# A hybrid attention and convolution layer: modulation rows, convolution taps and output products in another order, convolution sums in SBUF

## The reference, cut to what matters

```python
sc = silu(c)
mod = sc @ ada_w + ada_b
sh1, sc1, g1, sh2, sc2, g2 = split(mod, 6)
xn = rmsnorm(x, norm1_g) * (1.0 + sc1) + sh1
q, k, v, ca, cg = split(xn @ w_in)                     # 8 heads x 64, 512 conv channels
q, k = rmsnorm(q, q_norm_g), rmsnorm(k, k_norm_g)      # per head
y_attn = causal softmax(q k^T / 8 + rel_bias) v        # SEQ = 256: one block, all of it causal
a = causal_dwconv(ca * sigmoid(cg), conv_dw_w, conv_dw_b)   # 31 taps
a = silu(group_norm(a, conv_norm_g, conv_norm_b, 8))
x = x + g1 * (concat([y_attn, a]) @ w_out)
xn2 = rmsnorm(x, norm2_g) * (1.0 + sc2) + sh2
h = causal_dwconv(xn2 @ w_up, ffn_dw_w, ffn_dw_b)      # 3 taps
x = x + g2 * ((silu(h_gate) * h_up) @ w_down)
```

## Time and profile before

| what | us |
|---|---|
| median of 3 runs | 378.6 |
| lowest and highest run | 375.11, 380.57 |
| the profiled execution | 376.77 |
| its span in the trace | 375.0 |
| TensorE matmul busy | 352.2 (94%) |
| VectorE busy | 269.3 (72%) |
| ScalarE busy | 176.5 (47%) |

### The profile page before, as it was taken

One profiled execution on the slowest core, in us unless ns is written; L12 is line 12 of the kernel. 1 busy time (PEld: TensorE's weight loads), 2 busy tenths in 40 slices (PEclk: granted clock), 3 DMA queues, 4 the chain that ended last, 5 costly groups with the idle time before them and its releaser, 6 DMA issues.

```text
span 375.0 us, 6095 instructions
## 1 busy us (share of the span) xinstructions
PE 352.2 (94%) x2410; PEld 295.2 (79%) x2410; DVE 269.3 (72%) x489; ACT 176.5 (47%) x255; POOL 25.8 (7%) x67
## 2 busy tenths in 40 slices
PE   6789898999399989999899999999999999999995
PEld 5558877997046427776899899998989899999984
DVE  2654699999995547766968786768576667658665
ACT  4354635154003454946756563645554644636430
POOL 5371000000000200002300000000000000000000
PEclk9999999999889789999999999999999999999999
DMA  7999977698583576462326465544635545510003
GB/s 284 427 419 418 425 292 296 244 360 348 239 309 141 219 315 251 142 207 101 114 114 225 140 239 191 217 170 169 225 126 211 191 152 218 179 50 0 3 0 112
DMA packets 12797, 79.51 MB, mean 212 GB/s; under 512 B 1368, under 2 KB 2784, under 8 KB 3552
## 3 DMA queue, kind: packets, MB, share of 16 engines
q1 hardware_dynamic: 12560, 78.97, 55.8%
q10 hardware_dynamic: 144, 0.13, 0.1%
q0 software_dynamic: 64, 0.01, 0.0%
HBM read 78.05 MB, written 1.06 MB: 211 GB/s over the span
## 4 chain that ended last, share of the span: by engine, by line
PE 71%; DVE 17%; DMA 6%; ACT 2%; issue 1%; SPq 1%; POOL 0%; DVEq 0%; ACTq 0%; POOLq 0%
PE bank L883 20%; PE bank L884 19%; PE bank L885 19%; DVE bank L651 10%; DMA raw<-in_stream 6%; DVE w_lo L559 4%; PE bank L905 3%; PE bank L941 2%; PE bank L1144 2%; PE bank L1164 1%; PE bank L1154 1%; PE bank L1066 1%; PE bank L1171 1%; PE bank L955 1%; ACT w_hi L349 1%
## 5 line engine op out<-in xcount | busy, mean ns | idle before, releaser
L883 PE MATMUL bank<-act_hi,w_hi 128*128 128x256 f32 x480 | 137.3, 286 | 5.7 <-DVE glu L660 1.9
L884 PE MATMUL bank<-act_lo,w_hi 128*128 128x256 f32 x480 | 135.7, 283 | 0.0
L885 PE MATMUL bank<-act_hi,w_lo 128*128 128x256 f32 x480 | 135.7, 283 | 0.0
L559 DVE TENSOR_TENSOR w_lo<-raw,w_hi 128x2048 fp32r<-128x2048 f32 x45 | 103.6, 2301 | 27.8 <-ACT w_hi L349 27.8
L883 PEld LDWEIGHTS bank<-act_hi,w_hi 128*128 128x128 f32 x480 | 91.8, 191 | 13.6 <-issue 9.6
L884 PEld LDWEIGHTS bank<-act_lo,w_hi 128*128 128x128 f32 x480 | 91.9, 192 | 0.4
L885 PEld LDWEIGHTS bank<-act_hi,w_lo 128*128 128x128 f32 x480 | 91.9, 191 | 0.0
L349 ACT ACTIVATE w_hi<-raw 128x2048 fp32r<-128x2048 f32 x45 | 85.8, 1907 | 12.9 <-DMA raw<-in_stream 11.8
L651 DVE SCALAR_TENSOR_TENSOR bank<-glu,cols,bank 128x256 f32<-128x256 f32 x116 | 46.1, 474 | 0.0
L519 ACT ACTIVATE bias<-bank,cols 128x256 f32<-128x256 f32 x44 | 22.2, 556 | 34.4 <-PE bank L885 34.4
L883 PE MATMUL bank<-w_hi,hid_hi 128*128 128x512 f32 x88 | 34.8, 396 | 0.0
(11 more groups left out here) (164 smaller groups left out, 349.0 us busy)
## 6 DMA issues: line engine op xcount, KB each, us to landing
raw<-in_stream SPq DMA_DIRECT2D x71, 1024.0 KB, 5.0
xt<-in_x_t SPq DMA_DIRECT2D x2, 512.0 KB, 4.6
bias<-toeplitz_rows SPq DMA_DIRECT2D x1, 1024.0 KB, 10.8
xr<-in_x_rows SPq DMA_DIRECT2D x1, 1024.0 KB, 7.9
out<-xmod SPq DMA_DIRECT2D x3, 256.0 KB, 2.1
gates_b<-in_ada_b_gates SPq DMA_DIRECT2D x1, 256.0 KB, 8.4
cols<-in_cols SPq DMA_DIRECT2D x1, 185.0 KB, 5.4
out<-xmod SPq DMA_DIRECT2D x1, 128.0 KB, 1.9
```

What stands on the lines that cost most here:

```text
L559: nc.vector.tensor_tensor(w_lo[:, m % PARTS, :], slot(*SPLIT[m]), w_hi[:, m % PARTS, :].bitcast(f32), ALU.subtract).then_inc(lo_done, 1)
L883: nc.tensor.matmul(o, sh, mh, start=first, stop=False)
L884: nc.tensor.matmul(o, sh, ml, start=False, stop=False)
L885: return nc.tensor.matmul(o, sl, mh, start=False, stop=last)
```

## The change

It does six things.

1. The stream has two modulation rows behind each of conv 2 to qk 3: by the end of qk 3 TensorE has made rows 8 to 19 and not 8 to 14. Rows 20 and 21 lie among the v pieces (ADA_IN_V), rows 22 and 23 in head 0 (ADA_AT_HEAD and its call ahead of the loop). The gate biases are loaded behind conv 3 and not behind qk 3.
2. The convolution's sums are in SBUF (`conv`) from the first tap on.
3. VectorE makes 13 taps a tile and not 14, 2 and 10 around `qk_rstd`, and the last 21 in heads 0 to 3 (2, 8, 6, 5).
4. The gate rows are summed within the tile loop (at qk 2), spread on TensorE ahead of the v pieces and copied by ScalarE. `qk_spread` uses four banks.
5. The group norm: the mean of tiles 0 and 1 at the start, of tiles 2 and 3 one at a time in heads 4 and 5; squares and roots in head 6, spreading in head 7, scale and swish behind head 7.
6. The output products go in the order of the tiles 0 to 7: part 0 in heads 2 and 3, part 1 in head 4, part 2 in head 6, parts 3 to 7 behind head 7. The split of out 0 moves to head 0, that of out 1 to head 3; up 0 and up 1 are rounded and split behind head 7, ahead of the gated mixer.

```diff
-ADA_AFTER = {("conv", 2): 1, ("conv", 3): 1, ("qk", 0): 1, ("qk", 1): 1, ("qk", 2): 1, ("qk", 3): 2}
-ADA_AT_HEAD = (2, 2, 1)
+ADA_AFTER = {("conv", 2): 2, ("conv", 3): 2, ("qk", 0): 2, ("qk", 1): 2, ("qk", 2): 2, ("qk", 3): 2}
+ADA_IN_V = (1, 1)
+ADA_AT_HEAD = (1, 1)
+TAPS_A_TILE = 13
+TAPS_AT_HEAD = (2, 8, 6)
...
-OUT_TILES = [0, 1, 4, 5, 6, 7, 2, 3]
+OUT_TILES = list(range(KT))
...
         def conv_sum(j):
-            return bank[CONV_BANK[j // 2]][:, (j % 2) * SEQ:(j % 2) * SEQ + SEQ]
+            return conv[:, j, :]
...
-        HIGH_AT_HEAD = {0: SP_AT["out", 0], 2: SP_AT["out", 1], 4: SP_AT["out", 2], 5: SP_AT["out", 3], 6: SP_AT["up", 0]}
-        LOW_AT_HEAD = {1: SP_AT["out", 0], 4: SP_AT["out", 1], 5: SP_AT["out", 2], 6: SP_AT["out", 3], 7: SP_AT["up", 0]}
+        HIGH_AT_HEAD = {0: SP_AT["out", 0], 2: SP_AT["out", 1], 4: SP_AT["out", 2], 5: SP_AT["out", 3]}
+        LOW_AT_HEAD = {0: SP_AT["out", 0], 3: SP_AT["out", 1], 5: SP_AT["out", 2], 6: SP_AT["out", 3]}
...
-                if (kind, i) == ("qk", 3):
+                if (kind, i) == ("conv", 3):
                     sp.dma_start(gates_b[:, :], ada_b_gates).then_inc(gates_b_ready, 16)
...
             for h in range(HEADS):
                 normalise(h)
-                if h == 4:
-                    gn_scale()
+                if 1 <= h < HEADS - 1:
+                    add_bias(h + 1)
+                if h % 2 == 0 and h >= 2:
+                    att_lo_part(h // 2 - 1)
                 if h == 0:
-                    gn_centre(0)
-                    gn_centre(1)
...
+                    gn_centre_pair()
+                elif h == 2:
+                    norm2_columns()
+                elif h == 4:
+                    gn_centre(2)
+                elif h == 5:
+                    gn_centre(3)
+                elif h == 6:
                     dve.wait_ge(gn_std, 1)
                     nc.vector.reciprocal(gn_inv[:, :], gn_stat[:, :]).then_inc(gn_inverted, 1)
...
                 if h in LOW_AT_HEAD:
                     split_lo(LOW_AT_HEAD[h])
+                if h < len(TAPS_AT_HEAD):
+                    taps(TAPS_AT_HEAD[h])
+                elif h == len(TAPS_AT_HEAD):
+                    taps(len(TAPS))
+            gn_scale()
             att_lo_part(CT - 1)
+            mix_parts()
+            split_lo(SP_AT["up", 0])
+            split_lo(SP_AT["up", 1])
...
             x2_diagonal(1)
-            split_lo(SP_AT["up", 1])
...
                 head_turn(h)
                 if h == 0:
...
+                    late_ada(ADA_AT_HEAD[1])
+                    pe.wait_ge(v_ready, ST)
                 elif h == 2:
...
+                    pe.wait_ge(mod_rows_ready, 2)
+                    turn_mod_rows(7)
+                    pe.wait_ge(gn_centred, 1)
+                    out_part(0, [0, 1, 2])
                 elif h == 3:
...
+                    pe.wait_ge(mod_cols_read, 2)
+                    out_part(0, [3])
+                elif h == 4:
+                    out_part(1, [0])
+                    gn_mean_of(2)
+                    out_part(1, [1, 2, 3]).then_inc(w_used, 1)
+                    pe.wait_ge(gn_centred, 2)
+                elif h == 5:
+                    gn_mean_of(3)
+                    pe.wait_ge(gn_centred, 3)
+                elif h == 6:
+                    out_part(2)
+                    gn_turn()
+                elif h == 7:
                     gn_spread()
...
+            out_part(3).then_inc(w_used, 1)
+            out_part(4)
+            out_part(5).then_inc(w_used, 1)
             for t in range(ST):
                 out_part(6, [2 * t, 2 * t + 1])
```

More of the change, by code:

```diff
@@ L416, in after @@
                     if i == CT - 1:
+                        for n, b in enumerate((3, 5)):
+                            act.wait_ge(gate_bc, n + 1)
+                            nc.scalar.activation(gate[:, 0, n * 512:n * 512 + 512], bank[b][:, :], ACT.Copy).then_inc(gate_ready, 1)
                         act.wait_ge(qk_ssq, CT)
@@ L1012, in _, with late_ada @@
             ada_at = [KT]
+            def late_ada(n):
+                for _ in range(n):
+                    ada(ada_at[0], 2 if ada_at[0] < 2 * KT else 7)
+                    ada_at[0] += 1
             def later_ada(after):
-                for _ in range(ADA_AFTER.get(after, 0)):
-                    ada(ada_at[0], 2)
-                    ada_at[0] += 1
+                late_ada(ADA_AFTER.get(after, 0))
             for j in range(FIRST, CT):
```

189 lines of the change are left out of this document (77 added, 112 removed).

## The result

The changed kernel takes 403.3 us (399.0 to 406.6, 4 runs) where the kernel before takes 377.4 (375.1 to 380.6) on the same chip: a ratio of 1.058 with an interval of 1.052 to 1.065. Medians here are of all executions, while ratios leave out those more than 1.5% above the fastest of their kernel, here two of the four (406.4 and 406.6 us at a mean granted clock of 0.918, against 399.0 and 400.2 at 0.946 and 0.942). So the median is 16 us above the forecast and 9 above the upper end of the range, and the two shorter executions, at 399.6 on average, are 12 and 5 us above them. The direction was right.

A forecast was written before the change was run, and what follows sets the result against it. It took VectorE (conv and qk tiles, behind loads), the heads and the way to the first up product as bounds. 376.8 + 4.9 (to first scores) + 4.8 (heads) + 1.2 (tail) = 387.7, stated as 387.5 us; range 378 to 394.5.

The forecast's parts named there:

- (a): Up to the first scores: qk 0 is place 16 of the stream, not 14, with gate biases ahead: 5.5 us later.
- (b): Up to the first scores: 91 instead of 98 taps stand ahead of qk_inv, at 0.392 us each: -2.7 us.
- (c): Up to the first scores: the sum into gates_b (672 ns) moves ahead of qk_inv: +0.6 us.
- (d): Up to the first scores: VectorE waits for later loads, 3.9 us at qk 3 and 1.0 at v 0.
- Loads in time: Rival, chance 0.11: waits at qk 3 and v 0 don't come (-4.9), group norm hides (-3.2): 379.5 us.
- (e): From qk_inv to the first scores: 14.0 us, where the kernel before took 17.4.
- Heads: First scores to last output product: 63.0 us against 58.2 before, +4.8, with VectorE setting the pace from head 1.
- a rival at 0.17: Heads: idle TensorE falls to 1.2 GHz, another 14 us of work at half speed, +7: 394.5 us; chance 0.17.
- Tail: Last output product to first up product: mixer starts 2.0 us late behind up 1's split, 0.8 saved: +1.2 us.
- clock case: Heads: TensorE at 1.2 GHz for output parts 0 to 2 and the group norm, +7: 394.5 us; chance 0.17.
- load case: Loads catch up, so waits at qk 3 and v 0 vanish and group norm hides: 379.5 us; chance 0.11.
- Slower: Whole kernel: a time over 386.2 us, 2% above the median before; chance 0.55.

The follow-up runs named there:

- b_two: The kernel before with two modulation rows behind conv 2 and conv 3, one behind qk 0 to qk 2, none behind qk 3: 382.1 us, ratio 1.015.
- b_fewer: The kernel before with one modulation row less behind conv 2, used with the v products instead: 374.9 us, ratio 0.993.
- a_taps_first: The changed kernel with all 21 taps of heads 0 to 3 moved ahead of the first q and k normalisation: 397.4 us, ratio 1.054.
- a_no_gn: The changed kernel without the group norm's deviation (squares, roots, turning, spreading, scaling); swish reads the centred tiles: 392.8 us, ratio 1.041.
- a_one_row: The changed kernel with one modulation row instead of two behind conv 2 and conv 3, the two rows moved to the heads: 392.9 us, ratio 1.046.
- a_keep2: The changed kernel with matmuls that nobody reads put into TensorE's waits at many places: 393.6 us, ratio 1.043.
- a_keep_gn: a_keep2 without the group norm's squares, deviation, turning, spreading and scaling: 389.3 us, ratio 1.034.
- a_back: a_keep2 with two splits put back, out 0's behind head 1 and up 1's behind the diagonals: 392.4 us, ratio 1.042.
- b_fewer7: b_fewer with seven slots instead of six in the ring of weight loads: 375.5 us, ratio 0.992.

## Why the prediction was right and wrong

**(a) qk 0 two places later, +5.5: right.** Its split starts at 53.3 against 47.7, +5.6; b_two (+5.0) and b_fewer (-2.2, until the wait is gone) show the same rule in both directions.

**(b), (c) Taps and the gates sum, -2.1: right.** Tap pitch 0.39 (13 taps in 5.23 us with the last one's overlap), gates sum 0.68.

**(d) The later loads, +4.9: too small, the second step that failed.** Behind qk 0's split VectorE waits 9.8 us for loads in the profiled execution, and 6.6 and 7.7 us with the same instructions in a_taps_first and a_no_gn. qk 1's split at 63.1 was as said, qk 2's at 72.1 for 70.8, qk 3's at 80.1 for 79.8; v 0's came at 93.4 for 88.1 (90.0 and 91.4 in the other two). One part is in all three. I took 5.0 us and two places, 9.9, from the issue of the load behind ada 14 to v 0's landing. It took 11.1 to 11.4. The 5.0 of the earlier trace rows is the median of all 71 loads, and I had read it as that of a load issued alone. The other part depends on the execution. I had "TensorE ends qk 1 at 74.9" and "ada 14 used at 76.3". In a_taps_first that holds (76.6). In the profiled execution TensorE waits 2.05 us at 70.99 for the second glu, which I had in the sum for qk 0 and not for qk 1, runs at 1.2 GHz for 3.4 us and frees the slot at 80.3. 4.0 us of that and 1.2 of the load make up the 5.1 us that qk_inv is late by there; in a_taps_first and a_no_gn it is late by 1.7 and 3.1. The rival "Loads in time" erred further in the same direction.

**(e) qk_inv to first scores, 14.0: right in one execution, 2.8 short in the profiled one.** I took the clock of the kernel before (0.82 over 17.0 us) behind a wait that by my own sum had grown to 6.6 us. It was 7.12 us, and 0.62 over 16.4 followed; in a_no_gn it was 7.20, and 0.80 and 13.5 us followed. So the length of the wait alone doesn't decide it, and what does stays open. My upper bound for this step was 14.9.

**Heads, 63.0: the step that failed most, 8.7 us.** The order of the waits was right, but the sum priced all of TensorE's new stretches there at the full clock, though by its own words it left TensorE some 14 us idle; the low clock was a rival at 0.17 and no term. Measured were 71.7 us with 31 of them at 1.2 GHz (granted clock 0.78 and 0.79), against 7 in the kernel before: 24 more, where the rival had 14. It isn't the long execution alone: a_one_row, with a mean clock of 0.949 over the whole, takes 71.0. In a_keep2, with the clock at 1.00 there, VectorE's normalise stands 9.7, 14.3, 18.9 and 25.2 us behind the first scores for heads 1 to 4 (9.7, 14.3, 19.0 and 25.0 forecast) and head 5's values end at 35.3 (35). Then head 7's normalise is at 44.5 for 42.7, the last values at 50.2 for 47.7, and the rest takes 16.4 for 15.3: 3.6 us in all, of which a_keep_gn puts 0.9 down to the group norm (4.1 against 3.2). The others may be clock as well, for it was 0.50 from 162 to 166 us, at part 2. The 5.1 us between the change and a_keep2 are what the fillers gave. One claim of the sum holds only as a place, not as a price: head 1's late normalise behind out 0's split costs nothing by itself (a_back).

**Tail, +1.2: sum right (8.4 in a_keep2 for 8.0), then 1.8 of clock.** The diagonals' matmuls ran mostly at 1.2 GHz (6.62 us for 4.14) behind a wait of 2.43 us.

Added up: 5.1 + 2.8 + 8.7 + 2.2 = 18.8, which is 404.7 less my 385.9. About 11 of these are clock (1.5 in qk 1, 2.8, 5.1, 1.8), and the other 8 are waits and what the sum had too small. In the shortest execution, 7.5 us shorter, the miss is 11.3. It has no trace, but the nearest ones say where the miss may lie: first scores 2.5 us late (a_no_gn), heads 8.0 (a_one_row, which has two rows more there), tail 2.2.

**The range** held 378 to 394.5 because I treated the causes as exclusive: a clock case of +7 in the heads alone, a load case that could only get better. They add, and in the profiled execution one brings on the other: low clock from 20 us on, a later row, a later load, a wait of TensorE, low clock again. Two executions of the changed kernel give a price for the clock, if nothing else differs between them: 404.7 us at a mean of 0.918 and 397.2 at 0.946, that is 66 and 43 us at 1.2 GHz, 0.32 us lost for each such microsecond. The two ends of b_fewer7's executions (369.0 at 0.989, 378.1 at 0.962) give 0.44. "Slower" at 0.55 was too timid: nothing in the sum of terms pointed the other way.

## What to carry to other kernels

When weights stream through a ring in use order, look at which engine frees the slot of each load: a place ahead of the first late tile costs its full transfer until the wait is gone, and a slot that waits for the product of a late tile makes every following tile later. Follow every product's own waits, not only the first one's: whether the second one comes can hang on a clock that fell some 45 us earlier. Where a change opens waits on TensorE, put a price for the low clock behind them into the forecast, not only into a rival to it. And before a late instruction in a trace is explained, look at a second trace with the same instructions up to there: here 3.5 us of the lateness of v 0 were in one execution and not in the other.
